# A hybrid decoder layer: weights stored in load order, and a quarter of the MLP input by seven block products

## The reference, cut to what matters

```python
h = rms_norm(x, pre_norm_mix)
y = hybrid_mixer(h, w_in, conv_w, ..., w_branch_att, w_branch_dn, w_out)
x = x + rms_norm(y, post_norm_mix)
h = rms_norm(x, pre_norm_mlp)
y = square(relu(h @ w_mlp_in)) @ w_mlp_out      # 1024 x 4096, then 4096 x 1024
x = x + rms_norm(y, post_norm_mlp)
```

## Time and profile before

| what | us |
| --- | --- |
| median of 3 runs | 749.59 |
| lowest and highest | 749.42, 749.9 |
| the profiled execution, its own time | 749.34 |
| its span | 747.6 |
| TensorE matmuls busy | 740.2 |
| TensorE weight loads busy | 607.8 |
| VectorE busy | 435.5 |
| ScalarE busy | 389.5 |
| POOL busy | 324.9 |

### The profile page before, as it was taken

The page is one execution under the profiler, slowest core; times in us unless marked ns, Lnnn a source line. Parts: engine busy times, 40 slices in busy tenths (PEclk is TensorE's granted clock), DMA queues, the critical chain, the costliest instruction groups (busy, mean ns, idle before and its releaser), DMA issues.

```text
span 747.6 us, 11913 instructions
## 1 busy us (share of the span) xinstructions
PE 740.2 (99%) x4168; PEld 607.8 (81%) x4168; DVE 435.5 (58%) x651; ACT 389.5 (52%) x632; POOL 324.9 (43%) x296
## 2 busy tenths in 40 slices
PE   9999999999999999999999999999999999999996
PEld 7788778888877878788888988888888888888885
DVE  5897899980454545444983512221221777778795
ACT  6657842268554365635655733333332655555671
POOL 2348894435454754574536466546545000000002
PEclk9999999999999999999999999999999999999999
DMA  9436224456476597276650279979978575554652
GB/s 330 113 87 211 57 71 114 127 128 150 132 171 156 169 198 197 64 160 202 210 185 28 85 233 274 238 227 294 237 227 216 159 228 194 198 184 154 220 174 114
DMA packets 86302, 129.22 MB, mean 173 GB/s; under 512 B 6096, under 2 KB 45168, under 8 KB 86256
## 3 DMA queue, kind: packets, MB, share of 16 engines
q1 hardware_dynamic: 76384, 109.47, 45.8%
q0 software_dynamic: 9536, 18.88, 14.8%
q10 hardware_dynamic: 336, 0.28, 0.1%
HBM read 126.49 MB, written 39.86 MB: 223 GB/s over the span
## 4 chain that ended last, share of the span: by engine, by line
PE 93%; POOL 3%; ACT 2%; DVE 1%; DMA 0%; issue 0%; SPq 0%; POOLq 0%; ACTq 0%; DVEq 0%
PE bank L767 28%; PE bank L768 27%; PE bank L769 27%; POOL rsq L2167 2%; PE bank L1014 1%; PE bank L1037 1%; PE bank L1024 1%; POOL w_lo L2173 1%; PE bank L978 1%; PE bank L788 1%; PE bank L942 1%; PE bank L794 1%; PE bank L989 1%; PE bank L797 0%; PE bank L1076 0%; DMA raw<-in_w_in 0%
## 5 line engine op out<-in xcount | busy, mean ns | idle before, releaser
L2173 POOL TENSOR_TENSOR w_lo<-raw,w_hi 128x512 fp32r<-128x512 f32 x169 | 219.4, 1308 | 232.7 <-ACT w_hi L1229 230.7
L1229 ACT ACTIVATE w_hi<-raw 128x512 fp32r<-128x512 f32 (+2 forms) x214 | 145.1, 684 | 154.6 <-PE bank L769 126.5
L767 PE MATMUL bank<-h_hi,w_hi 128*128 128x512 f32 (+1 forms) x528 | 208.6, 395 | 0.2
L768 PE MATMUL bank<-h_lo,w_hi 128*128 128x512 f32 (+1 forms) x528 | 204.2, 387 | 0.0
L769 PE MATMUL bank<-h_hi,w_lo 128*128 128x512 f32 (+1 forms) x528 | 204.1, 387 | 0.0
L767 PEld LDWEIGHTS bank<-h_hi,w_hi 128*128 128x128 f32 x528 | 99.2, 188 | 26.1 <-issue 5.1
L769 PEld LDWEIGHTS bank<-h_hi,w_lo 128*128 128x128 f32 x528 | 99.2, 188 | 20.5
L768 PEld LDWEIGHTS bank<-h_lo,w_hi 128*128 128x128 f32 x528 | 99.3, 188 | 18.6
L1638 DVE SCALAR_TENSOR_TENSOR relu_sb<-bank,rs_row 128x512 f32<-128x512 f32 x32 | 20.6, 686 | 126.5 <-PE bank L769 114.8
L2311 POOL TENSOR_SCALAR ssh<-ssy 128x1 f32<-128x1 f32 x4 | 1.0, 238 | 151.6 <-ACT junk L1609 151.6
L767 PE MATMUL bank<-w_hi,a_hi 128*128 128x512 f32 x120 | 46.8, 390 | 0.0
(11 more groups left out here) (327 smaller groups left out, 1268.0 us busy)
## 6 DMA issues: line engine op xcount, KB each, us to landing
raw<-in_w_in SPq DMA_DIRECT2D x87, 256.0 KB, 2.9
raw<-in_w_mlp_in SPq DMA_DIRECT2D x62, 256.0 KB, 4.9
t_sum<-in_w_mlp_out POOLq DMA_DIRECT2D x12, 1024.0 KB, 10.7
raw<-in_w_mlp_out SPq DMA_DIRECT2D x26, 256.0 KB, 3.1
raw<-t_sum SPq DMA_DIRECT2D x26, 256.0 KB, 3.2
v_sum<-in_w_mlp_out SPq DMA_DIRECT2D x4, 1024.0 KB, 6.5
t_sum<-in_w_mlp_out SPq DMA_DIRECT2D x4, 1024.0 KB, 7.2
v_sum<-in_w_mlp_out POOLq DMA_DIRECT2D x4, 1024.0 KB, 11.4
```

Of the source, the lines that this page charges most:

```text
L767: pe.matmul(o, s_hi, m_hi, start=start, stop=False, skip_group_check=True)
L768: pe.matmul(o, s_hi, m_lo, start=False, stop=False, skip_group_check=True)
L1229: return a.activation(o, i_, ACT.Copy, scale=scale)
L2173: g.tensor_tensor(w_lo[:, slot, :], raw[:, slot, :], w_hi[:, slot, :].bitcast(F32), ALU.subtract).then_inc(lo_ready, 1)
```

## The change

Three things at once.

**Layout.** The host lays `w_in`, the two branch matrices, `w_mlp_in` and `w_mlp_out` out in DRAM unit by unit, so that a load reads 128 contiguous rows of 2 KB. The blocks of the DRAM sums become contiguous too; copies and adds of 1 MB are described as 128 rows of 8 KB.

**Seven products for the last quarter of the MLP input.** The first 12 groups stay (`G_PLAIN`). The last 1024 MLP features are computed against 1024 inputs and 512 tokens as 2 by 2 blocks (two halves of the inputs, two of the tokens, two of the features) in `STEPS_IN` = 2 steps of seven products `q1 q6 q5 q2 q7 q3 q4`, each of two units; a unit is 12 matmuls of 256 columns. So 28 units take the place of 16. The activation side (`h_full`, `t_full`, `ts_hi`, `ts_lo`) is made during groups 4 to 7 on VectorE and ScalarE. Results are combined through `p1`, `e1`, `f1` and `relu_sb` by VectorE, with ScalarE's copies of `p1`; the waits on `made_in` and `p1_copied` order this. Of 14 units of a step POOL makes 4 low parts and VectorE 10. The loads go through a ring of 8 buffers (four new ones and the four of `raw`).

**Sums.** The weight side of these products needs four more sums of 1 MB (`u_sum`), copies behind units 48, 52, 56 and 64, adds two units later. The copies of the sums for the output projection and the MLP output move to later units (tables below). One copy and two adds of the last chain now fall into the steps. As the new tiles lie over `x_res` and `pn_mlp`, x2 is stored to DRAM during groups 2 and 3 and loaded back, with `pn_mlp`, by POOL's queue in the output product.

```diff
-U_M1 = U_OUT + 64
+G_PLAIN = 12
+F_HALF = (FF - G_PLAIN * 256) // 2
+U_S = U_OUT + 4 * G_PLAIN
+STEPS_IN = F_HALF // 256
+PER_STEP = 14
+RING = 8
+CHUNKS = F_HALF // 512
+U_M1 = U_S + STEPS_IN * PER_STEP
...
-OUT_SUM_AT = {48: 0, 52: 1, 60: 2, 87: 3}
+OUT_SUM_AT = {60: 0, 67: 1, 74: 2, 90: 3}
...
-SUM_AT = {61: (0, 0), 65: (1, 0), 73: (2, 0), 74: (0, 1), 78: (1, 1), 86: (2, 1)}
+SUM_AT = {70: (0, 0), 77: (1, 0), 81: (2, 0), 82: (0, 1), 86: (1, 1), 95: (2, 1)}
...
-SUM_IN = {2: (0, 2), 3: (0, 3), 4: (3, 0), 5: (3, 1), 7: (2, 2), 8: (2, 3), 9: (1, 2), 10: (1, 3), 12: (3, 2), 13: (3, 3)}
+IN_SUM_AT = {48: (0, 0), 52: (1, 0), 56: (2, 0), 64: (3, 0)}
+SUM_IN = {2: (0, 2), 3: (0, 3), 4: (3, 0), 5: (3, 1), 7: (2, 2), 8: (2, 3), 9: (1, 2), 10: (1, 3), 11: (3, 2)}
+IN_PRODUCTS = ("q1", "q6", "q5", "q2", "q7", "q3", "q4")
+IN_BANK = {"q1": 0, "q2": 0, "q6": 2, "q7": 2, "q4": 2, "q5": 4, "q3": 4}
+LOW_POOL = (1, 3, 7, 11)
+LOW_DVE = tuple(v for v in range(PER_STEP) if v not in LOW_POOL)
```

On SP, behind the plain groups:

```diff
+                if g in (2, 3) and j % 2:
+                    t = 2 * (g - 2) + j // 2
+                    if t == 0:
+                        sp_.wait_ge(*x2_signal(2))
+                        sp_.wait_ge(*x2_signal(3))
+                    sp_.dma_start(x2_copy[t], x_res[:, t, :]).then_inc(copied_out, 16)
...
+        for s in range(STEPS_IN):
+            for v in range(PER_STEP):
+                u = U_S + PER_STEP * s + v
+                if v >= RING - RAW or s:
+                    sp_.wait_ge(*low_of(u - RING))
+                sp_.dma_start(raw_of(u), in_source(s, v)).then_inc(raw_signal(u)[0], 16)
+                if (s, v) == (1, 0):
+                    sp_.wait_ge(*added(3, 3))
+                    sp_.dma_start(*t_copy(3, 3)).then_inc(t_copied[3], 16)
```

On TensorE:

```diff
-        with pe.Fori(1, 8) as i:
+        with pe.Fori(1, G_PLAIN // 2) as i:
             mlp_in(i, False)
+        def in_product(s, name):
...
+            elif name == "q4":
+                pe.wait_ge(made_in, made("c22", s, 1))
...
+            for half in range(2):
+                u = U_S + PER_STEP * s + 2 * IN_PRODUCTS.index(name) + half
+                pe.wait_ge(*low_of(u))
+                for kk in range(2):
+                    for e in range(2):
+                        c = slice(kk * 256 + e * P, kk * 256 + e * P + P)
+                        x_ = three(bank[IN_BANK[name] + e][:, 0:256], w_hi[:, u % SPL, c], w_lo[:, u % SPL, c],
+                                   *in_operand(name, 2 * half + kk), ...)
+                x_.then_inc(unit_done, 1)
```

On ScalarE:

```diff
+        def split_in(u):
+            a.wait_ge(*raw_signal(u))
+            a.wait_ge(unit_done, u - 3)
+            copy(w_hi[:, u % 4, :], raw_of(u)).then_inc(hi_ready, 1)
```

On VectorE, in `step_in(s)`, where `v_` is the unit of the step:

```diff
+                if v_ == 10:
+                    v.wait_ge(unit_done, u)
+                    v.wait_ge(made_in, made("f", s, 1))
+                    for e in range(2):
+                        v.tensor_tensor(relu_sb[:, 2 * e + 1, 256:512], bank[2 + e][:, 0:256], f1[:, e, :], ALU.subtract).then_inc(made_in, 1)
...
+                in_low(u + LEAD)
+                if v_ in (7, 9):
+                    combine_in(G_PLAIN - 2 + 2 * s + v_ // 2 - 3)
```

On POOL:

```diff
+                if v in LOW_POOL:
+                    g.wait_ge(hi_ready, nth(u))
+                    g.tensor_tensor(w_lo[:, u % 4, :], raw_of(u), w_hi[:, u % 4, :].bitcast(F32),
+                                    ALU.subtract).then_inc(lo_ready, 1)
+                if (s, v) == (0, 1):
+                    add_sum(3, 2)
+                if (s, v) == (1, 7):
+                    add_sum(3, 3)
+        g.wait_ge(part_done, 16)
+        for t in range(NT):
+            g.dma_start(x_res[:, t, :], x2_copy[t]).then_inc(late_in, 16)
+        g.dma_start(pn_mlp[:], post_norm_mlp[0].partition_broadcast(P)).then_inc(late_in, 16)
```

More of the change, by code:

```diff
@@ L187, in loads, with made @@
     return u // 4 + 1 - (1 if u >= U_X and u % 4 >= 2 else 0)
+def made(name, s, e):
+    return 14 * s + 2 * ("e1", "f", "c11", "c22", "c12", "c21", "relu").index(name) + e + 1
 STEPS = side_steps()
@@ L732, in _ @@
         one(1, range(2, 8))
-        with sp_.Fori(2, NI) as i:
+        with sp_.Fori(2, 6) as i:
             one(i)
-        sp_.wait_ge(t_added[3], 16 * N_SUM)
+        with sp_.Fori(6, NI) as i:
+            one(i)
+        sp_.wait_ge(*added(3, N_SUM))
         two(0, S_TWO - 8)
@@ new lines, in split_in, with mlp_in_last @@
+        def split_in(u):
+            a.wait_ge(*raw_signal(u))
+            a.wait_ge(unit_done, u - 3)
+            copy(w_hi[:, u % 4, :], raw_of(u)).then_inc(hi_ready, 1)
+        def mlp_in_last(i):
+            for j in range(8):
+                u = U_OUT + LEAD + 8 * i + j
+                if u < U_S:
+                    split(None, u % 4, 16 * loads(u), u - 3)
+                else:
+                    split_in(u)
+                if j in (3, 7):
+                    square_group(i, j // 4)
@@ new lines, in square_in, with mlp_in_step @@
+        def square_in(s, e):
+            a.wait_ge(made_in, made("relu", s, e))
+            for m in range(2):
+                a.activation(act_pair(G_PLAIN + 2 * s + e, slice(4, 6) if m else slice(0, 3, 2)),
+                             relu_sb[:, 2 * e + m, :].rearrange("p (s c) -> p s c", s=2), ACT.Square).then_inc(act_ready, 1)
+        def mlp_in_step(s):
+            for v in range(PER_STEP):
+                u = U_S + PER_STEP * s + v
+                if u + LEAD < U_M1:
+                    split_in(u + LEAD)
+                else:
+                    a.wait_ge(unit_done, u)
+                    w_split(u + LEAD - U_M1, 1, 16)
+                if v == 2:
+                    if s:
+                        a.wait_ge(made_in, made("c21", s - 1, 1))
+                    for e in range(2):
+                        copy(p1[:, e, :], bank[e][:, 0:256]).then_inc(p1_copied, 1)
+                if s and v in (3, 4):
+                    square_in(s - 1, v - 3)
+                if s == STEPS_IN - 1 and v == 8:
+                    a_split(0, 0, slice(0, 4))
@@ L1553, in _ @@
         a_split(1, 1, slice(0, 4))
-        square_group(NI - 1, 1)
         w_split(6, 2, 16)
+        for e in range(2):
+            square_in(STEPS_IN - 1, e)
         with a.Fori(1, NI - 1) as i:
@@ L2060, in _ @@
         a_low(1, 1, slice(0, 4), 2)
+        for e in range(2):
+            relu_in(STEPS_IN - 1, e)
         w_low(6, 2, 8)
```

361 lines of the change are left out of this document (275 added, 86 removed).

## The result

| what | before | after |
| --- | --- | --- |
| median, us | 749.81 | 847.61 |
| lowest and highest | 749.42, 750.42 | 844.8, 849.02 |
| runs | 5 | 5 |
| profiled execution, own time | 749.34 | 847.94 |
| its span | 747.6 | 846.2 |

What follows compares the result with a forecast made beforehand. TensorE's matmul count times spacing was taken as the bound, all else being covered: 749.59 - 3.2 (seven products) + 0.6 (stalls) = 747.0 us, with layout and new DMAs at 0. Range 746.1 to 751.2 us.

Steps and rivals of the forecast that it cites:

- The new DMAs: Eight 1 MB copies and adds of input-weight sums, units 48 to 66: taken as 0, at worst a few us.
- 5.9 us for an added MB: Price of accumulating DMA traffic on all engines, from the queue lines: 111 us for 18.9 MB of adds.
- Wrong altogether: Sign that the forecast fails entirely: matmul spacing other than 0.120, or new waits before microsecond 400.
- Rival C: DMA late in the steps, load 15 behind SP's wait for an add: 752.4 us; chance 0.08 within 0.2%, 0.12 slower.
- 192 x 0.2267 into 336 x 0.1200: TensorE in the last MLP-input quarter: matmul count times spacing falls from 43.5 to 40.3 us, gaining 3.2 us.
- Rival D: Waits between products break the 0.1200 spacing in the steps, costing 2.8 us: 749.2 us; chance 0.02.
- Layout 0, between 0 and -0.2: Load-order weights with 2 KB rows and moved sums: taken as 0, between 0 and -0.2 us.
- no load ends a wait, so this is worth nothing: Layout step's check: no load ends a TensorE wait today, so the longer rows gain nothing by themselves.
- Stalls of 0.6 in the steps: TensorE waits in the two seven-product steps: 0.6 us taken, between bounds of 0 and some 2.6 us.
- first tight place: Step's start: ScalarE's leftover squares, then a split and POOL's low part, take 4.1 of 4.3 us available.
- as before: Sign that the forecast is right: the tail unchanged from the last matmul on.
- Rival B: VectorE and POOL block each other at c22 and POOL's low parts in both steps, 2 to 3 us: 749.0; chance 0.12.

Runs made afterwards that it cites:

- e1: Changed kernel with all eight input-weight sum DMAs (copies and adds) listing the dimension of 64 outermost instead of 2; 752.34 us, ratio 1.0038.
- e8: e1 plus last-step squares moved behind the output loop's first pass, MLP-output adds in 2 KB rows, two copy-and-add pairs moved; 749.93 us, ratio 1.0006.
- e9: e8 plus SP's border raw_c loads put first and POOL's third wo_lo waiting for VectorE's four h_lo; 747.63 us, ratio 0.9975.
- e4: Kernel before with the new DRAM layout alone, no seven products or input sums; 749.89 us, ratio 1.0.
- e12: Kernel before with its 16 MLP-output adds listing 4 blocks outermost instead of 128 partitions; 802.29 us.
- e2: As e1, but 64 outermost for the four adds only, the copies left at 2; 772.47 us.
- e3: As e1, but 64 outermost for the four copies only, the adds left at 2; 818.47 us.

## Why the prediction was wrong

- **The new DMAs, "I take 0; the other end is a few us".** This is the step that failed. It priced a transfer by its megabytes on all 16 engines, from the earlier trace rows, and asked only whether the share had room. Room there was, in e1 0.69. The price per MB holds for the shape that the old DMAs have, and the new ones have another, in a line of code that the change adds. They were served by 2 engines (share 0.13), so the prediction's own 5.9 us for an added MB becomes 47, and 44 to 60 were measured. The step had also left out that two of the copies wait on SP for adds, with all loads of the input projection behind them. A bound could have come from the trace: if an add lands n times as late, SP waits for that long less the gap to the copy that needs it, and only the lead of three units (some 8 us) covers that. Measured, in place of 0 to a few us: 95 us.
- **"Wrong altogether: ... new waits before microsecond 400."** That is what the list of waits and the slices show. None of the rivals had this mechanism; C had a late DMA, but in the steps and at 6 us.
- **192 x 0.2267 into 336 x 0.1200.** Right. In e8 the steps last 40.3 us, the forecast's figure to the tenth, and up to the output product e9 is ahead by 2.95 us of the 3.2. The gap of 262 cycles that the Trainium skill (TensorE: Matmul & The Clock Gate, Back-to-back issue gap) has for an isolated matmul would have given an estimated 36.7 for them; the runs go by the trace's spacing. (A slip without effect: 40.3 less 38.1 is 2.2, not 2.3.) Rival D, broken spacing, didn't occur.
- **Layout 0, between 0 and -0.2.** Right for the time (e4), but the range left out its other sign. POOL's work moved onto VectorE's, 0.9 us of wait. The check "no load ends a wait, so this is worth nothing" holds for gains only.
- **Stalls of 0.6 in the steps.** In e1 0.8 us of waits there, so nearly right, and at the first tight place that it names: a low part of POOL at the step's start, behind a split that ScalarE made late, after squares. It is one profile, and e8 has no such wait. But 3.8 us came at three borders: 0.7 for `h_lo`, 0.7 for the last plain groups, 2.4 for `a_lo` behind the steps. The prediction had looked for squares at the start of the first step, where they fitted, and wrote of the tail "as before"; the squares of the last step stood at the start of the output product.
- **Rival B, the shared port.** The mechanism is real and was worked out from the earlier trace rows, but TensorE never waited for c22, and POOL's low part behind e1's 0.8 us took its usual 1.28 us, so it was late and not stretched. The port cost at `wo_lo`, which the change doesn't touch.
- **Rival C, the late add ahead of load 15.** SP stood 2.5 us for it in e1, within the forecast of 2 to 4, and load 15 was not late for TensorE.

Had the pattern been right, the forecast would still have been missed, 752.34 being 1.1 above its range. What was right in size was what can be counted, matmuls by spacing; what was off were the hand-overs at borders between stages.

## What to carry to other kernels

Read a DMA's access pattern as the hardware gets it, outermost dimension first, before its bytes are priced: two dimensions in the wrong order turned 10 us into 50 for an add here, while rows and bytes were the same. The trace shows it where one such DMA is alone: its mean share of the DMA engines gives the number that serve it, 0.13 for 2 of 16 here. A sum or copy that one queue waits for shares the fate of everything behind it on that queue, so a new wait on the load queue wants a bound from the loads' lead, not from bandwidth. And where stage B begins with work that the last part of stage A leaves over, walk through that border as closely as through the stage itself.

## What was not expected of the hardware

- A 1 MB accumulating DMA lands after 9.4 to 11.9 us with 64 outermost (e1) and after 44 to 60 with 2; with 4 after 29 to 32 where the stretch is otherwise as before (e12).
- An add with 2 outermost is served by 2 of the 16 DMA engines (share 0.13, 28 GB/s, where it is nearly alone), and packets of loads alternate with its 0.63 us pieces there. A copy with the same 2 outermost, but both sides unbroken in DRAM, is through in 4 to 6 us.
- Slow copies on SP's queue delay the loads issued after them: from 135 to 250 us the median landing goes from 2.8 to 6.8 us, the longest from 9.7 to 25.6 (e1, e2), though the loads have 128 rows outermost. Slow adds on POOL's queue do so too: 9.8 in the median in e3 (135 to 340 us, 3.3 in e1), and 10.3 instead of 4.9 for `w_mlp_in` in e12.
- POOL's issue of an add costs 0.96 us with the good order and 1.37 with the bad one for the same bytes and rows, 0.80 with 128 rows of 8 KB (e1, L2617), and 1.9 us in e12 after 1.23.
- An earlier start of POOL's work can make TensorE wait: VectorE operations of 0.7 us beside it took 1.7 (e4). The Trainium skill (SBUF — State Buffer, SBUF: two separate sides) describes this lock for a VectorE operation with two SBUF inputs against a GpSimd one; the rows of e4 agree, with 1.0 us lost each time.
